# Expert blocks of 32 rows as four column groups in a one-core decoder trunk step

## The chip, the core and the metric

The kernel runs on one core of one Trainium2 chip. The time is the device time of that core in microseconds (us). Every product here is in f32; the trace shows each f32 product as two MATMUL records, so counts of records are twice the counts in the code.

## What is computed

One inference step of a decoder layer for 512 prompt tokens and 8 sample tokens (520 rows of 1024): a gated recurrent branch and a linear-attention branch, a merge, a layer norm, and then a mixture of experts. The change concerns the mixture alone:

```python
grp_logits = h @ w_grp + b_grp;  g_sel = argmax(grp_logits)          # 4 groups
sel_logits = (h @ w_exp + b_exp).reshape(N, 4, 8)[n, g_sel]          # 8 experts in the group
top_v, top_i = lax.top_k(sel_logits, 2)
e_id = g_sel * 8 + top_i;  e_w = softmax(top_v) * softmax(grp_logits)[g_sel]
y = sum over the 2 experts:  e_w * ((silu(h @ we_gate[e]) * (h @ we_up[e])) @ we_down[e])
```

There are 32 experts, with gate and up weights of 1024x512 and down weights of 512x1024, so 2 MB each and 6 MB an expert. 520 tokens make 1040 pairs of token and expert. With the reference's inputs its router gives the experts these counts, in order: 29, 84, 12, 7, 45, 22, 68, 117, 52, 33, 64, 10, 61, 60, 15, 19, 10, 7, 14, 8, 28, 15, 32, 24, 10, 29, 40, 10, 23, 44, 22, 26.

## The kernel before

The first part (projections, recurrences, merge, output projection, router) runs job by job, and the change leaves it alone up to the router's plan. VectorE then counts the pairs of each expert, cuts them into blocks of at most `CAP` rows, and gives each pair a block and a place in it. TensorE turns that into a table `idx` with one matmul per tile and choice (job `table`): for each block and place, which row of `hf_scratch` to gather and which row of `pair_scratch` to write. A second small job (`plan`) makes the table `plan` of register values: for each block the half of the weight ring that it uses and how many loads must have landed; for each load the expert and the block after which its slot is free.

The expert stage is a loop written for all engines, two blocks to an iteration (`two_blocks`), with `NBLK // 2` iterations; iterations past the last block fall through their `If`s. The count of blocks is in a register `n`. For a block b in slot j = b % 2 of all double buffers:

- GpSimd (`gather`) fetches the rows of block b + 2 by an indirect DMA into `xg[j]`, and (`scatter`) writes the result `yb[j]` of an earlier block to `pair_scratch`.
- TensorE, in this order: `gate_up(b)`, both products into one bank of PSUM; `transpose_rows` of block b + 1; `finish(b - 1)`, which calls `down`; the transposes of the product `act` of block b.
- ScalarE: silu of the gate, the copy of the transposed rows to `xT` for block b + 1, the copy of the transposed product to `acT`.
- VectorE: the product with the up half into `act`, and the copy of a result out of PSUM (`take_result`).
- The SP queue loads weights (`load_expert`) into a ring of two slots of three tiles. Expert e takes slot e % 2: gate and up wait until the last block of expert e - 2 is through `gate_up`, down until it is through `down`. SP works this list in order.

Before each `gate_up` and again before each `down` TensorE's own sequencer reads three values of `plan` for the block (`weights_of`), waits for the loads that they name, and takes one of two branches by the slot:

```python
lies, in0, in1 = weights_of(i * 2 + j)
for m in range(2):
    pe.wait_ge(we_in[m], in0 * 16)
    pe.wait_ge(we_in[3 + m], in1 * 16)
for slot in range(2):
    with pe.If(lies < 1 if slot == 0 else lies > 0):
        gate_up(j, slot)
```

In a block of 64 rows each of the two products of `gate_up` has 64 columns of the array to itself: gate goes to partitions 0 to 63 of the bank, up to 64 to 127, and `down` lays the two halves of its 1024 outputs in the same way. After the loop SP reads `pair_scratch` back, and the last layer norm follows.

## Time and profile before

| | us |
|---|---|
| median of 3 runs | 1518.23 (1515.2 to 1527.52) |
| span of the profiled execution, its own time in the trace | 1523.0 |
| first `gate_up` starts | 880.38 |
| last `down` ends | 1453.56 |

The trace has times from the start of the span. For the profiled execution there is no other time than its span; it lies between the highest run and the median. A row of TensorE in the timeline gives the start and the length of a run of instructions of one line, their count, and in square brackets how long the engine was idle before it and what ended that. Rows with PEldq are instructions of TensorE's sequencer (branches, register loads, waits), which are not counted as busy.

### The profile page before, as it was taken

To read this page: it belongs to the slowest core of one execution; us is meant where nothing else is said; L and a number is where in the kernel's file an instruction comes from. 1 tells how busy PE (TensorE), PEld (TensorE's weight loads), DVE (VectorE), ACT (ScalarE), POOL (GpSimd) and SP (SyncE) were. 2 spreads that over 40 slices of the span, in tenths; PEclk is the share of its full clock that TensorE was granted. 3 is DMA by queue.
4 is the path that set the end of the run, shared out by engine and by line. 5 is a ranking of instruction groups with operands and counts; after the bars stand their busy time and mean duration, and the time that the engine had idled before them with its cause. 6 is when DMAs were issued, how large, how long until landed. Compare 5 with 4: busy or idle time off the path is not lost.

```text
span 1523.0 us, 18481 instructions
## 1 busy us (share of the span) xinstructions
PE 1262.4 (83%) x6402; PEld 815.4 (54%) x6403; DVE 413.6 (27%) x704; ACT 307.3 (20%) x433; POOL 127.0 (8%) x203
## 2 busy tenths in 40 slices
PE   3899999999999999999987379798887977788710
PEld 3687878787878888888643223233332332233300
DVE  3326240423332260010386601111111111111156
ACT  3255550410000320000100012121211111111221
POOL 0100000000000000000000111111111111111134
PEclk9899999998878999999998579999998999889965
DMA  8744412124232213413003457996999999999631
GB/s 286 238 171 157 176 56 69 48 72 151 83 110 70 84 56 114 165 56 111 31 15 155 193 194 299 389 348 262 396 397 379 393 367 394 383 378 391 259 119 55
DMA packets 69930, 307.24 MB, mean 202 GB/s; under 512 B 10039, under 2 KB 18744, under 8 KB 56917
## 3 DMA queue, kind: packets, MB, share of 16 engines
q1 hardware_dynamic: 59786, 294.77, 50.5%
q0 software_dynamic: 6272, 10.14, 2.1%
q10 hardware_dynamic: 3820, 1.60, 0.4%
q8 instruction: 38, 0.62, 0.2%
q14 instruction: 14, 0.11, 0.0%
HBM read 298.35 MB, written 18.55 MB: 208 GB/s over the span
## 4 chain that ended last, share of the span: by engine, by line
PE 64%; DMA 18%; DVE 8%; issue 4%; ACT 3%; SPq 2%; ACTq 0%; POOL 0%; POOLq 0%; DVEq 0%; PEldq 0%
PE ps L1482 33%; DMA mem<-in_we_up 13%; PE ps L1750 12%; PE ps L1759 5%; PE ps L1709 3%; DMA mem<-in_w_mod 2%; PE ps L1639 2%; PE ps L1742 2%; PE ps L1636 1%; PE ps L1621 1%; DVE mem L1445 1%; PE ps L1647 1%; DMA mem<-in_we_gate 1%; DVE mem L1444 1%; PE ps L1515 1%
## 5 line engine op out<-in xcount | busy, mean ns | idle before, releaser
L1482 PE MATMUL ps<-mem 128*128 128x260 f32 (+1 forms) x2336 | 546.6, 396 | 10.3 <-ACT mem L813 3.9
L1482 PEld LDWEIGHTS ps<-mem 128*128 128x128 f32 (+1 forms) x2336 | 454.5, 196 | 95.3 <-issue 12.6
L1750 PE MATMUL ps<-mem 128*64 128x512 f32 x1120 | 286.7, 671 | 99.9 <-DMA mem<-in_we_up 78.4
L1750 PEld LDWEIGHTS ps<-mem 128*64 128x64 f32 x1120 | 89.7, 154 | 270.9 <-issue 270.9
L1424 DVE TENSOR_TENSOR mem<-mem,ps 64x512 f32<-64x512 f32 x35 | 24.1, 690 | 431.3 <-ACT mem L1002 431.3
L1759 PE MATMUL ps<-mem 128*64 128x512 f32 x560 | 129.2, 604 | 3.4 <-issue 3.4
L1002 ACT ACT_TABLE_LOAD x35 | 44.9, 1283 | 372.5 <-PE ps L1750 372.5
L1759 PEld LDWEIGHTS ps<-mem 128*64 128x64 f32 x560 | 37.5, 138 | 66.8 <-issue 64.5
L710 POOL DMA_INDIRECT pair_scratch<-mem x35 | 32.7, 934 | 458.2 <-DVE mem L1416 458.2
L1416 DVE COPY mem<-ps 64x512 f32<-64x512 f32 x70 | 48.1, 688 | 78.1 <-PE ps L1759 77.0
L1709 PE MATMUL ps<-mem 128*128 128x512 f32 x128 | 59.8, 628 | 0.0
L1742 PEld LDWEIGHTS ps<-mem 64*128 64x128 f32 x288 | 34.4, 200 | 32.6 <-issue 32.6
L931 ACT ACTIVATE mem<-ps,mem 128x520 f32<-128x520 f32 x16 | 11.1, 694 | 169.9 <-PE ps L1482 169.8
L1742 PE MATMUL ps<-mem 64*128 64x64 f32 x288 | 39.4, 278 | 4.0 <-DMA mem<-hf_scratch,mem 4.0
L651 POOL IOTA mem<- 128x4 int32 x1 | 0.1, 137 | 510.0 <-DVEq L1218 510.0
L1709 PEld LDWEIGHTS ps<-mem 128*128 128x128 f32 x128 | 25.4, 201 | 31.7 <-issue 31.6
L688 POOL DMA_INDIRECT mem<-hf_scratch,mem x37 | 35.9, 970 | 31.5 <-POOL mem L719 29.7
L1814 PEld LDWEIGHTS ps<-mem 64*128 64x128 f32 x140 | 19.4, 210 | 29.5 <-issue 29.5
L1238 DVE TENSOR_TENSOR mem<-mem,ps 128x520 f32<-128x520 f32 x8 | 5.6, 696 | 102.9 <-PE ps L1482 102.9
L906 ACT ACTIVATE mem<-ps,mem 128x520 f32<-128x520 f32 x8 | 5.6, 694 | 133.8 <-PE ps L1482 133.8
L1009 ACT ACTIVATE mem<-ps 128x256 f32<-128x256 f32 x35 | 13.5, 384 | 94.0 <-PE ps L1814 94.0
L1515 PE MATMUL ps<-mem 128*9 128x128 f32 x768 | 25.9, 292 | 5.2 <-DMA mem<-in_w_mod 5.2
(284 smaller groups left out, 988.7 us busy)
## 6 DMA issues: line engine op xcount, KB each, us to landing
mem<-in_we_gate SPq DMA_DIRECT2D x32, 2048.0 KB, 12.0
mem<-in_we_up SPq DMA_DIRECT2D x32, 2048.0 KB, 16.5
mem<-in_we_down SPq DMA_DIRECT2D x32, 2048.0 KB, 8.9
mem<-in_w_in SPq DMA_DIRECT2D x14, 2048.0 KB, 8.5
mem<-in_w_mod SPq DMA_DIRECT2D x12, 2048.0 KB, 12.0
out<-mem SPq DMA_DIRECT2D x13, 512.0 KB, 5.3
mem<-in_state_gla SPq DMA_DIRECT2D x8, 512.0 KB, 3.9
mem<-v_scratch SPq DMA_DIRECT2D x8, 512.0 KB, 4.3
```

The source lines that it names most:

```text
L688: pool.indirect_dma_start(xg[j][0:CAP, :], None, hf_dram, bass.IndirectOffsetOnAxis(ap=gidx[j][0:CAP, 0:1], axis=0), bounds_check=NT - 1, ...
L710: pool.indirect_dma_start(pair_dram, bass.IndirectOffsetOnAxis(ap=sidx[j][0:CAP, 0:1], axis=0), yb[j][0:CAP, :], None, bounds_check=PAIRS ...
L1002: sc.activation(sg[j][CAP:2 * CAP, :], ps[0:CAP, 2 + j, :], ACT.Silu).then_inc(sg_ready[j], 1)
L1416: v.tensor_copy(yb[j][0:CAP, q * 512:(q + 1) * 512], ps[CAP * q:CAP * q + CAP, 4 + j, :])\
L1424: v.tensor_tensor(act[j][0:CAP, :], sg[j][CAP:2 * CAP, :], ps[CAP:2 * CAP, 2 + j, :], ALU.mult)\
L1482: ins = pe.matmul(out[0:m, h, 0:HALF], w[:, k, col:col + m], src[:, k, h * HALF:(h + 1) * HALF], start=(k == 0), stop=(k == KD - 1))
L1515: pe.matmul(o, cs[:, k, :], w[:, k, g * P:(g + 1) * P], start=(k == 0), stop=False)
L1639: ins = pe.matmul(o, S[n % 2][:, h, d * P:(d + 1) * P], Q[:, h, cols], start=False, stop=True)
L1709: ins = pe.matmul(out[0:r, h, :], Z[:, k, i * P:i * P + r], wo[h][:, k, :], start=(k == 0), stop=(k == KD - 1))
L1742: ins = pe.transpose(ps[:, j, k * CAP:(k + 1) * CAP], xg[j][0:CAP, :].rearrange("s (p k) -> s k p", k=KD)[:, k, :], ident[0:CAP, 0:CAP])
L1750: ins = pe.matmul(ps[CAP * q:CAP * q + CAP, 2 + j, :], xT[j][:, k, :], ring[3 * slot + q][:, k, :], start=(k == 0), stop=(k == KD - 1))
L1759: ins = pe.matmul(ps[CAP * q:CAP * q + CAP, 4 + j, :], acT[j][:, k, :], wd[:, k, q * 512:(q + 1) * 512], start=(k == 0), stop=(k == 3))
```

## The change

A block has 32 rows instead of 64, the program is built for up to 64 blocks instead of 48, and SPLITS, the number of thresholds of the block count, goes from 9 to 17. In `gate_up` four column groups of 32 take a half of gate or up each (256 outputs), in `down` a quarter of the 1024 outputs each. Gathered rows lie as quarters: partition 32q + s holds quarter q (256 values) of row s, so `xg` and `yb` fill 128 partitions with 1 KB each, and the table repeats the indices for the four quarters (`piece` adds q). Two full transposes replace eight smaller ones, and two replace four for the product. The order of the rows of the weight tiles follows from that: a partition holds, of gate and up, four pieces of 4 KB that lie 512 KB apart in memory, and of down two pieces of 8 KB that lie 1 MB apart; before it held 16 KB in one piece.

```diff
-CAP = 64
+CAP = 32
+Q4 = 4
+DQ = D // Q4
+HE = DE // 2
-NBLK = 48
+NBLK = 64
-SPLITS = 9
+SPLITS = 17
...
-                to = ring[3 * slot + m]
-                if m < 2:
-                    sp.dma_start(to, w.rearrange("o (p k) n -> p (o k) n", p=P)).then_inc(we_in[3 * slot + m], 16)
-                else:
-                    sp.dma_start(to.rearrange("p k n -> p (k n)"), w.rearrange("o (p k) n -> p (o k n)", p=P))\
-                      .then_inc(we_in[3 * slot + m], 16)
+                to = ring[3 * slot + m].rearrange("p k n -> p (k n)")
+                q = Q4 if m < 2 else 2
+                sp.dma_start(to.rearrange("p (q w) -> p q w", q=q),
+                             w.rearrange("o (q p h) n -> p (o q) (h n)", q=q, p=P)).then_inc(we_in[3 * slot + m], 16)
...
-                pool.indirect_dma_start(xg[j][0:CAP, :], None, hf_dram,
-                                        bass.IndirectOffsetOnAxis(ap=gidx[j][0:CAP, 0:1], axis=0),
-                                        bounds_check=NT - 1, oob_is_err=False).then_inc(xg_in[j], 16)
+                pool.indirect_dma_start(xg[j][:], None, hf_dram.rearrange("t (q e) -> (t q) e", q=Q4),
+                                        bass.IndirectOffsetOnAxis(ap=gidx[j][:, 0:1], axis=0),
+                                        bounds_check=Q4 * NT - 1, oob_is_err=False).then_inc(xg_in[j], 16)
...
-                        sc.activation(sg[j][CAP:2 * CAP, :], ps[0:CAP, 2 + j, :], ACT.Silu).then_inc(sg_ready[j], 1)
+                        sc.activation(sg[j][2 * CAP:P, :], ps[0:2 * CAP, 2 + j, 0:HE], ACT.Silu).then_inc(sg_ready[j], 1)
...
-                for q in range(2):
-                    v.tensor_copy(yb[j][0:CAP, q * 512:(q + 1) * 512], ps[CAP * q:CAP * q + CAP, 4 + j, :])\
-                     .then_inc(y_ready[j], 1)
+                v.tensor_copy(yb[j][:], ps[:, 4 + j, 0:DQ]).then_inc(y_ready[j], 1)
...
-                ins = pe.matmul(out[0:CAP, 0, 0:2 * NBLK], place_oh[0:r, n, :], named[0:r, n].rearrange("p b c -> p (b c)"),
-                                start=(n == 0), stop=(n == 2 * TILES - 1))
+                for q in range(Q4):
+                    ins = pe.matmul(out[CAP * q:CAP * q + CAP, 0, 0:2 * NBLK], place_oh[0:r, n, :],
+                                    named[0:r, n].rearrange("p b c -> p (b c)"), start=(n == 0), stop=(n == 2 * TILES - 1))
...
-                for k in range(KD):
-                    for q in range(2):
-                        ins = pe.matmul(ps[CAP * q:CAP * q + CAP, 2 + j, :], xT[j][:, k, :], ring[3 * slot + q][:, k, :],
+                for h in range(2):
+                    ins = pe.transpose(ps[:, j, h * P:(h + 1) * P], xg[j].rearrange("s (p h) -> s h p", h=2)[:, h, :], ident[:])
+                ins.then_inc(xt_done[j], 1)
+
+            def gate_up(j, slot):
+
+                for k in range(KD):
+                    for q in range(Q4):
+                        ins = pe.matmul(ps[CAP * q:CAP * q + CAP, 2 + j, 0:HE], xT[j][:, k % 2, CAP * (k // 2):CAP * (k // 2) + CAP],
+                                        ring[3 * slot + q // 2][:, k, (q % 2) * HE:(q % 2 + 1) * HE],
                                         start=(k == 0), stop=(k == KD - 1))
...
                 for k in range(4):
-                    for q in range(2):
-                        ins = pe.matmul(ps[CAP * q:CAP * q + CAP, 4 + j, :], acT[j][:, k, :],
-                                        wd[:, k, q * 512:(q + 1) * 512], start=(k == 0), stop=(k == 3))
+                    for q in range(Q4):
+                        ins = pe.matmul(ps[CAP * q:CAP * q + CAP, 4 + j, 0:DQ], acT[j][:, k % 2, CAP * (k // 2):CAP * (k // 2) + CAP],
+                                        wd[:, k, q * DQ:(q + 1) * DQ], start=(k == 0), stop=(k == 3))
```

Three places show how the order on an engine changes. Lines of the changed kernel are a few higher than those of the kernel before. The first is TensorE in the loop, from the branch into `gate_up` of a block to the branch into `finish`. Before:

```order
L1796 COMPARE_AND_BRANCH
L1750 MATMUL ps<-mem 64x512 x16
L1796 UNCONDITIONAL_BRANCH
L1799 ISA
L1742 MATMUL ps<-mem 128x64 x8
L1788 UNCONDITIONAL_BRANCH
L1804 COMPARE_AND_BRANCH
```

The same place in the changed kernel:

```order
L1800 COMPARE_AND_BRANCH
L1753 MATMUL ps<-mem 32x256 x32
L1800 UNCONDITIONAL_BRANCH
L1803 ISA
L1746 MATMUL ps<-mem 128x128 x2
L1792 UNCONDITIONAL_BRANCH
L1808 COMPARE_AND_BRANCH
```

Sixteen matmuls of 64 columns become 32 of 32 columns and half the length, eight transposes become two, and the sequencer's own instructions stay. The second place is TensorE from the branch into `down` to the transposes of the product. Before:

```order
L1783 COMPARE_AND_BRANCH
L1759 MATMUL ps<-mem 64x512 x8
L1783 UNCONDITIONAL_BRANCH
L1809 COMPARE_AND_BRANCH
L1810 REGISTER_ALU
L1811 REGISTER_ALU
L1814 MATMUL ps<-mem 128x64 x4
```

In the changed kernel:

```order
L1787 COMPARE_AND_BRANCH
L1763 MATMUL ps<-mem 32x256 x16
L1787 UNCONDITIONAL_BRANCH
L1813 COMPARE_AND_BRANCH
L1814 REGISTER_ALU
L1815 REGISTER_ALU
L1818 MATMUL ps<-mem 128x64 x2
```

The matmuls of `down` double in number at half the length, the transposes halve in number. The third place is the SP queue, one expert's loads in the loop. Before:

```order
L587 ISA
L550 ISA
L550 DMA mem<-in_we_gate 128x4096
L550 DMA mem<-in_we_up 128x4096
L552 DMA mem<-in_we_down 128x4096
```

In the changed kernel:

```order
L589 ISA
L554 ISA
L554 DMA mem<-in_we_gate 128x4x1024
L554 DMA mem<-in_we_up 128x4x1024
L554 DMA mem<-in_we_down 128x2x2048
```

The loads stand in the same order with the same bytes, each partition's part now in four pieces or two.

## Rows read from the trace of the kernel before

**Rows 1.** Windows of the expert stage: us, busy us (instructions), granted clock, DMA share, GB/s.

```profile
880.38:1144.99 264.61, 222.26 (x1005) 85.64 (x1005) 33.73 (x49) 48.52 (x68) 37.65 (x66) 0.93 0.85 332
1144.99:1346.17 201.18, 163.13 (x720) 62.00 (x721) 24.79 (x36) 34.25 (x48) 25.70 (x46) 0.90 0.94 380
1346.17:1453.56 107.39, 85.79 (x376) 32.35 (x376) 12.39 (x18) 18.41 (x25) 14.91 (x26) 0.90 0.80 322
```

**Rows 2.** Timeline of TensorE, one block and the start of the next.

```profile
1016.40 7.09 PE L1750 MATMUL ps<-mem 128*64 128x512 f32 x32 [1.44 <-issue]
1023.42 1.09 PE L1742 MATMUL ps<-mem 64*128 64x64 f32 x8
1024.44 3.65 PE L1759 MATMUL ps<-mem 128*64 128x512 f32 x16
1028.03 0.69 PE L1814 MATMUL ps<-mem 64*128 64x64 f32 x4
1030.54 8.78 PE L1750 MATMUL ps<-mem 128*64 128x512 f32 x32 [1.82 <-issue]
```

**Rows 3.** Sequencer of TensorE by line: ns, first and last start, same block.

```profile
L1799 PEldq FUSED_REGOPS  x1: 42/42/42, 1019.0 to 1019.0; - x1
...
L1804 PEldq COMPARE_BRANCH  x1: 71/71/71, 1020.8 to 1020.8; - x1
...
L1783 PEldq COMPARE_BRANCH  x2: 78/148/218, 1023.6 to 1024.5; - x2
...
L1811 PEldq ALU_OP  x2: 32/32/32, 1012.5 to 1026.2; - x2
```

**Rows 4.** ScalarE and VectorE in the same block, timeline.

```profile
1023.59 1.28 ACT L1002 ACT_TABLE_LOAD   x1 [8.13 <-PE ps L1750]
...
1025.51 0.69 DVE L1424 TENSOR_TENSOR mem<-mem,ps 64x512 f32<-64x512 f32 x1 [9.62 <-ACT mem L1002]
```

**Rows 5.** Sequencer of TensorE around one `down` of the other slot.

```profile
L1783 PEldq COMPARE_BRANCH  x2: 68/148/228, 1251.5 to 1251.8; - x2
...
L1809 PEldq COMPARE_BRANCH  x1: 71/71/71, 1252.4 to 1252.4; - x1
```

**Rows 6.** TensorE by line and form: the earlier matmul in four column groups.

```profile
L1704 PE MATMUL ps<-mem 128*8 128x256 f32 x64 | 3.6, 379 | 0.0
```

**Rows 7.** Timeline of TensorE, `gate_up` of six blocks.

```profile
880.38 9.22 PE L1750 MATMUL ps<-mem 128*64 128x512 f32 x32 [3.14 <-issue]
...
1144.99 10.03 PE L1750 MATMUL ps<-mem 128*64 128x512 f32 x32 [4.52 <-DMA mem<-in_we_up]
...
1161.91 7.09 PE L1750 MATMUL ps<-mem 128*64 128x512 f32 x32 [1.66 <-issue]
...
1194.33 8.78 PE L1750 MATMUL ps<-mem 128*64 128x512 f32 x32 [1.91 <-DMA mem<-in_we_up]
...
1346.17 7.09 PE L1750 MATMUL ps<-mem 128*64 128x512 f32 x32 [1.06 <-issue]
...
1431.37 8.50 PE L1750 MATMUL ps<-mem 128*64 128x512 f32 x32 [5.01 <-DMA mem<-in_we_up]
```

**Rows 8.** Before the stage: the table's matmuls, and one VectorE instruction of the plan.

```profile
864.33 0.83 DVE L1363 TENSOR_TENSOR mem<-mem 128x640 f32<-128x640 f32 x1
...
867.35 3.65 PE L1727 MATMUL ps<-mem 128*64 128x96 f32 x20 [9.52 <-DVEq L1369]
```

**Rows 9.** DMA in 830 to 845 (16 KB pieces), and in 575 to 580 (2 KB pieces of `p_a`).

```profile
DMA packets 475, 6.44 MB, mean 430 GB/s; under 512 B 48, under 2 KB 48, under 8 KB 93
...
DMA packets 952, 1.96 MB, mean 392 GB/s; under 512 B 1, under 2 KB 1, under 8 KB 951
```

**Rows 10.** The end of the stage: the last `down`, and VectorE's branches after its last block.

```profile
1448.55 5.01 PE L1759 MATMUL ps<-mem 128*64 128x512 f32 x16 [3.44 <-issue]
...
L1421 DVEq COMPARE_BRANCH  x12: 56/56/63, 1454.1 to 1460.9; - x12
```

**Rows 11.** DMA issues: the gathers, median us to landing.

```profile
mem<-hf_scratch,mem POOLq DMA_INDIRECT x37, 9.3
```

More of the change, by code:

```diff
@@ L215, in build @@
         hfT = [area(B + WT + 1024 * j, KD, P) for j in range(2)]
-        xT = [area(Z0 + 512 * j, KD, CAP) for j in range(2)]
-        sg = [area(Z0 + 1024 + 512 * j, DE) for j in range(2)]
-        act = [area(Z0 + 2048 + 512 * j, DE) for j in range(2)]
-        acT = [area(Z0 + 3072 + 256 * j, 4, CAP) for j in range(2)]
-        xg = [area(A0 + 4160 + 1024 * j, D) for j in range(2)]
-        yb = [area(A0 + 4160 + 2048 + 1024 * j, D) for j in range(2)]
+        xT = [area(Z0 + 256 * j, 2, P) for j in range(2)]
+        sg = [area(Z0 + 512 + 256 * j, HE) for j in range(2)]
+        act = [area(A0 + 4160 + 1024 + 256 * j, HE) for j in range(2)]
+        acT = [area(A0 + 4160 + 1536 + 128 * j, 2, 2 * CAP) for j in range(2)]
+        xg = [area(A0 + 4160 + DQ * j, DQ) for j in range(2)]
+        yb = [area(A0 + 4160 + 512 + DQ * j, DQ) for j in range(2)]
         ln2 = area(A0, 2, D)
@@ L261, in build @@
         fmv = keep(TILES, 4)
+        piece = keep(1)
         wa2 = area(2 * WT + 2048, 512)
@@ L316, in build @@
         place_oh = area(Z0 + 1024, 2 * TILES, CAP)
-        block_oh = area(Z0 + 1024 + 640, 2 * TILES, NBLK)
-        named = area(Z0 + 1024 + 1120, 2 * TILES, NBLK, 2)
-        idx = area(Z0 + 3584, TW, 2).bitcast(I32)
+        block_oh = area(Z0 + 1024 + 320, 2 * TILES, NBLK)
+        named = area(Z0 + 1024 + 960, 2 * TILES, NBLK, 2)
+        idx = area(Z0 + 3500, TW, 2).bitcast(I32)
         gidx = [area(Z0 + 3700 + j, 1).bitcast(I32) for j in range(2)]
@@ L679, in _ @@
             for j in range(2):
-                link(pool.memset(xg[j][0:CAP, :], 0.0))
+                link(pool.memset(xg[j][:], 0.0))
             pool.wait_ge(idx_ready, 1)
@@ L1392, in _ @@
             await_job(v, ("table", 0))
-            link(v.tensor_scalar_add(idx[0:CAP, 0:NBLK, :],
-                                     slot_banks(("table", 0))[0:CAP, 0, 0:2 * NBLK].rearrange("p (b c) -> p b c", c=2), float(OOB)))
-            link(v.tensor_scalar(idx[0:CAP, NBLK:TW, :], blk_f[0:CAP, 0:2 * (TW - NBLK)].rearrange("p (b c) -> p b c", c=2),
+            link(v.tensor_scalar(idx[:, 0:NBLK, :], slot_banks(("table", 0))[:, 0, 0:2 * NBLK].rearrange("p (b c) -> p b c", c=2),
+                                 piece[:, 0:1], 0.0, ALU.add, ALU.add))
+            link(v.tensor_scalar(idx[:, NBLK:TW, :], blk_f[:, 0:2 * (TW - NBLK)].rearrange("p (b c) -> p b c", c=2),
                                  0.0, float(OOB), ALU.mult, ALU.add))
@@ L1757, in down @@
                 for k in range(4):
-                    for q in range(2):
-                        ins = pe.matmul(ps[CAP * q:CAP * q + CAP, 4 + j, :], acT[j][:, k, :],
-                                        wd[:, k, q * 512:(q + 1) * 512], start=(k == 0), stop=(k == 3))
+                    for q in range(Q4):
+                        ins = pe.matmul(ps[CAP * q:CAP * q + CAP, 4 + j, 0:DQ], acT[j][:, k % 2, CAP * (k // 2):CAP * (k // 2) + CAP],
+                                        wd[:, k, q * DQ:(q + 1) * DQ], start=(k == 0), stop=(k == 3))
                 ins.then_inc(dn_done, 1)
@@ L1812, in two_blocks @@
                         pe.sem_inc(pe_turns, 1)
-                        for k in range(4):
-                            ins = pe.transpose(ps[:, 6 + j, k * CAP:(k + 1) * CAP],
-                                               act[j][0:CAP, :].rearrange("s (p k) -> s k p", k=4)[:, k, :],
-                                               ident[0:CAP, 0:CAP])
+                        for h in range(2):
+                            ins = pe.transpose(ps[:, 6 + j, 2 * CAP * h:2 * CAP * (h + 1)],
+                                               act[j][0:2 * CAP, :].rearrange("s (p h) -> s h p", h=2)[:, h, :],
+                                               ident[0:2 * CAP, 0:2 * CAP])
                         ins.then_inc(tr_done[j], 1)
```

32 lines of the change are left out of this document (16 added, 16 removed).

## The prediction

> **What bounds the kernel now.** The change sits in the expert stage, from 880.38 to 1453.56, so I read that stage first by windows, then the timeline of TensorE, then its sequencer. The windows [rows 1] show two regimes. In the middle one, 201.18 us for twelve experts of one block each, the DMA engines are 0.94 busy at 380 GB/s: 16.8 us an expert, and TensorE waits for weights. In the first window, 264.61 us for experts 0 to 13 in 17 blocks, DMA is only 0.85 busy, since three experts have two blocks and hold their slot longer.
>
> How long a block takes when its weights are there is seen in [rows 2]: `gate_up` starts at 1016.40 and the next at 1030.54, so 14.1 us, of which the array works 12.3 and then sits idle 1.82, with no engine named as the cause. The sequencer's rows [rows 3] show the cause. It passes L1811 at 1026.2, and the next `gate_up` starts 4.3 us later; on the iteration before, 1012.5 to 1016.40, it is 3.9. In that time it ends the `If`, loops, reads three registers and takes the branch. What it waits for at L1811 is ScalarE and VectorE: `gate_up` ends at 1023.5, the table load runs from 1023.59 for 1.28, VectorE ends at 1026.20 [rows 4]. So a block is `gate_up` 7.1, plus 2.7 for silu and product, plus 4.1 of sequencer: 13.9. The array's work on `down` and the transposes (1.09, 3.65 and 0.69 [rows 2]) lies beside that and sets nothing. The same register work stands ahead of `down`: from L1804 at 1020.8 to L1783 at 1023.6, 2.8 us [rows 3], today hidden because `gate_up` is long and the sequencer runs ahead of the array.
>
> **How many blocks.** From the router's counts, 64 rows make 35 blocks and 32 rows make 47. Experts 0 to 13 go from 17 to 27, experts 14 to 25 stay at 12, experts 26 to 31 go from 6 to 8. The bytes of weights stay.
>
> **The new block, step by step.** (1) `gate_up`. The nearest row is the earlier matmul in four groups with the same length: 64 records in 3.6 us [rows 6], so the groups do run side by side, 0.053 us a record, and 64 records here take about 3.65. Its groups have 8 columns, here 32; from the loads of 64 columns, which stay hidden today, I take no extra.
>
> (2) The clock. A `gate_up` after 1.66 us of idle ran at full clock in 7.09, after 1.91 in 8.78, after 1.82 also in 8.78 [rows 2, 7]. The extra is 1.7 there and 2.9 in the row of 10.03. If the new block idles longer than that before each `gate_up` (step 5 says 3 us), each one pays about 1.7: 5.35. Bounds: 3.65 with no drop, 7.0 if the clock never rises.
>
> (3) How far ahead the sequencer gets. At L1799, 2.6 us into `gate_up`, all 32 records are issued, and the array has 4.5 of 7.1 us left, which is 21 records of 0.22 us. So about 21 records is the lead. In the new block 21 records are 1.1 us: the sequencer leaves `gate_up` 4.1 us after its start, needs about 0.4 for two transposes, and is at the branch of `finish` at 4.5.
>
> (4) The 2.8 us of register work now start there and end at 7.3, when the array has been done for 1.5 us. Then 32 records of `down` are issued. In [rows 5] 16 records are issued between 1251.8 and 1252.4, at most 0.03 us each, so 1.0 here, and with the branch L1811 comes at 8.85. Silu and product are ready by then (5.35 + 2.35 = 7.7; the two instructions are half as long).
>
> (5) Then the 4.1 us as today: 12.95 us a block. The array ends `down` near 9.4 and the transposes near 9.9 and idles 3 us. With the clock up throughout the same steps give 11.25, with the clock always low 13.65. A block of 32 rows then costs nearly what one of 64 costs, because what is halved is the array's part, and the sequencer's part is the same for each.
>
> **The sum, against the span of 1523.0.**
>
> - Before the stage: the table gets 80 records for 20, in four groups; 20 records took 3.65 [rows 8]. Side by side that is about +0.8, and the longer plan instructions on VectorE about +0.9, from 0.83 for 640 elements [rows 8]; the first transposes and copy give back 0.8. Together +0.9 (0 to +4).
> - Experts 0 to 13: 27 x 12.95 = 350, plus one wait for weights early on of some 3, is 353 against 264.6: +88. DMA alone would need 12 x 16.5 = 198, so TensorE sets the pace and both slots are full ahead of it.
> - Experts 14 to 25: the first two find weights in the ring (13 and 15.6 us), then DMA binds again at about 16.6: 195 against 201.2, so -6. The 16.6 is today's 16.8 with two opposite terms. The hand-over is faster, which closes part of the 6% in which DMA idles. Against it stand smaller pieces: 16 KB pieces moved at 430 GB/s, 2 KB pieces at 392 [rows 9], so 4 and 8 KB pieces cost between 0 and 1.4 us an expert; I take 0.5. Bounds of this term: -16 to +8.
> - From the first block of expert 26 to the last `gate_up`, today 1346.17 to 1431.37: 7 x 12.95 plus one wait of 3.4, 94 against 85.2: +9.
> - The tail from the last `gate_up` to the last `down`: 22.2 today, of which 5.0 for `down` at low clock [rows 7, 10]. The shorter `gate_up` and `down` give about -3.6.
> - The loop's end: 8 empty iterations instead of 6 on VectorE. Six take 1454.1 to 1460.9, so 1.25 each [rows 10]; of 2.5 more some hides behind the last scatter, and one copy replaces two: +0.7 (0 to +2.5).
>
> Gathers and scatters move the same bytes in four times as many pieces. I cost them at nothing: a gather lands in 9.3 us [rows 11] and is issued about two blocks ahead, 26 us; if it took twice that, it would still be in time. GpSimd's order stays, and the vector copies are shorter.
>
> Sum: 0.9 + 88 - 6 + 9 - 3.6 + 0.7 = +89 on 1523.0, so 1612. The median stands 4.8 below that span, so I carry the difference over: 1518 + 89 = 1607, I say 1606.
>
> **The rivals.** *The sequencer hides* (8 in 100). If the register work still lay behind the array, a block would take the array's time with today's pause before `gate_up`: 3.65 + 0.5 + 1.85 + 0.5 + 1.7 = 8.2. Experts 0 to 13 would take about 250 (221 plus waits for weights at experts 4, 6 and 12 and their slow restarts), -14; experts 14 to 25 about -3; the rest about -9 with a shorter tail: 1492, faster. It decides below some 9.5 us a block. For it speaks that the pairing of groups works [rows 6]; against it the 2.8 and 4.1 us that have no wait in them [rows 3]. The Trainium skill, "TensorEngine Tiling (Array Packing)", in its section on theoretical speedup, puts the gain for a stationary side of at most 32 columns at up to four times, against two at 64. By that rule the array's part halves, which is this rival; the rows with the sequencer's part speak against taking it for the block.
>
> *The clock stays up* (19 in 100): 11.25 a block gives 27 x 1.7 = 46 less for the first stretch and 8 less at the end, 1552. Against it: 3 us of idle before each `gate_up`, where 1.9 was enough [rows 7]. *The clock never rises* (14 in 100): 0.7 more on 34 blocks, 1630. *The transfers slow down* (5 in 100): pieces that lie far apart cost more than small ones, 1 us an expert and more on the twelve that DMA sets and the waits near them, 1620 to 1630. The Trainium skill, "DMA: Bandwidth & Descriptors", under its latency and other measured facts, reports that rows at pitches of large powers of two read slower, somewhat at 512 KiB and more at 2 MiB and above. Here the pieces of a partition lie 512 KB apart; the pieces of `p_a` lie just so and moved at 392 GB/s [rows 9], so the trace speaks against it. *The groups don't run side by side* (2 in 100): `gate_up` of 32 columns would take 13.7 us, and the time would pass 1750.
>
> **How the numbers follow.** The forecast, 1585 to 1620 around 1606, has the other 52 in 100. A change of under 1% (15 us) can hardly be told from none with runs that spread by 12 us. Faster by over 1%, under 1503: 5 in 100, most of the first rival. Within 1%: 5, its upper part. Slower: 90. The range reaches from 1545, just below the case of the high clock, to 1632, the case of the low clock: outside lie the first rival, the last, and parts of two others.
>
> **What would show it.** In the changed kernel: 47 table loads for silu; `gate_up` near 5.3 us; between the xT transposes and `down` an idle stretch of 1.5 us or more, and some 3 us before the next `gate_up` where no weights are awaited; blocks 12 to 14 us apart in experts 6 to 13; DMA clearly less busy than 0.85 there and above 0.94 in experts 16 to 25. The prediction is wrong if blocks follow each other within 10 us, or if the idle stretches end with a gather or a weight load.

## The result, and the profile after

The changed kernel takes 1533.4 us (median of 6 runs, 1526.8 to 1536.7) against 1519.7 for the kernel before in the same job: a ratio of 1.0083, interval 1.0051 to 1.0114 (1.0090 by the two medians). Run again in a later job, it stood at 1533.9 against 1517.3, 1.013 (1.0102 to 1.0158). So it is slower, as forecast, but by 14 to 17 us where 88 were forecast.

The profiled executions alone would mislead. That of the changed kernel was the fastest of its six (span 1525.1), that of before lay above its median (span 1523.0), so the spans differ by only 2.1. The terms below come from these two; the profile of the second job is set beside them.

The stage by windows, as in [rows 1] (us, busy us of PE, PEld, DVE, ACT and POOL, granted clock, DMA share, GB/s): experts 0 to 13, 14 to 25, then the last ones up to the end of the last `down`, and ten of the one-block experts alone:

```profile
877.01:1169.24 292.23, 183.38 (x2668) 105.88 (x2669) 22.45 (x53) 62.67 (x108) 63.97 (x104) 0.95 0.79 310
1169.24:1354.43 185.19, 100.28 (x1201) 51.72 (x1201) 10.17 (x24) 27.85 (x48) 31.76 (x52) 0.79 1.01 404
1354.43:1452.93 98.50, 58.79 (x832) 32.71 (x832) 6.79 (x16) 19.07 (x33) 18.59 (x30) 0.92 0.87 340
...
1196.06:1354.43 158.37, 85.78 (x1001) 43.52 (x1001) 8.47 (x20) 23.21 (x40) 24.81 (x40) 0.78 1.02 411
```

The first window went from 264.6 to 292.2 us although TensorE works less in it (183 against 222). The second went from 201.2 to 185.2, at 404 GB/s against 380. One block, on TensorE's timeline (the answer to [rows 2]):

```profile
1084.19 3.66 PE L1753 MATMUL ps<-mem 128*32 128x256 f32 x64 [2.32 <-issue]
1087.79 0.50 PE L1746 MATMUL ps<-mem 128*128 128x128 f32 x2
1089.84 1.94 PE L1763 MATMUL ps<-mem 128*32 128x256 f32 x32 [1.55 <-DMA mem<-in_we_down]
1091.70 0.45 PE L1818 MATMUL ps<-mem 64*128 64x64 f32 x2
1094.30 3.66 PE L1753 MATMUL ps<-mem 128*32 128x256 f32 x64 [2.15 <-issue]
```

The array works 6.5 us of 10.1 and pauses twice: 1.55 before `down` and 2.15 before the next `gate_up`. The first pause is put down to a weight load, but the sequencer's rows of the same block (the answer to [rows 3]; in order of time: end of `gate_up`'s branch, branch of `finish`, branch ahead of `down`, wait for the product, branch ahead of the next `gate_up`) say what it is:

```profile
L1803 PEldq FUSED_REGOPS  x1: 42/42/42, 1086.4 to 1086.4; - x1
...
L1808 PEldq COMPARE_BRANCH  x1: 71/71/71, 1086.6 to 1086.6; - x1
...
L1787 PEldq COMPARE_BRANCH  x2: 68/142/217, 1089.4 to 1089.7; - x2
...
L1815 PEldq ALU_OP  x1: 32/32/32, 1090.5 to 1090.5; - x1
...
L1800 PEldq COMPARE_BRANCH  x1: 71/71/71, 1094.2 to 1094.2; - x1
```

The sequencer never rests: 2.2 us to issue `gate_up`, 0.2, 2.8 of register work, 1.1 with the issue of `down`, 3.8 to the next `gate_up`. VectorE ends the product at 1090.1, 0.4 us before L1815 asks for it:

```profile
1089.68 0.42 DVE L1427 TENSOR_TENSOR mem<-mem,ps 64x256 f32<-64x256 f32 x1 [7.61 <-ACT mem L1007]
```

So a block is as long as its instruction stream, 10.1 us. The product of [rows 4] was what the sequencer waited for before; it no longer is.

The clock is the surprise. `gate_up` of three blocks, with the idle time before each:

```profile
1012.15 3.66 PE L1753 MATMUL ps<-mem 128*32 128x256 f32 x64 [2.69 <-issue]
...
1115.25 5.35 PE L1753 MATMUL ps<-mem 128*32 128x256 f32 x64 [2.73 <-issue]
...
1196.06 6.45 PE L1753 MATMUL ps<-mem 128*32 128x256 f32 x64 [7.46 <-DMA mem<-in_we_up]
```

After 2.69 us of idle time the first ran at a granted clock of 1.00; the second, after nearly the same 2.73, at 0.68. In the kernel before, 1.82 us had been enough to slow a block [rows 2]. But its trace also has a block that stayed at full clock after 1.87:

```profile
940.16 7.09 PE L1750 MATMUL ps<-mem 128*64 128x512 f32 x32 [1.87 <-issue]
```

So even there the length of the pause did not put slow and fast blocks in order. Of the 27 blocks of experts 0 to 13 of the changed kernel only 5 are slow. In the profile of the second job 9 are, and that window takes 297.8 us: the same blocks, the same pauses, another draw of the clock.

The forecast's terms against these two traces (us):

| term | forecast | measured |
|---|---|---|
| planning, from the first rank matmuls to the first `gate_up` | +0.9 | +0.3 (25.2 to 25.5) |
| experts 0 to 13 | +88 | +27.6 (second profile +33.2) |
| experts 14 to 25 | -6 | -16.0 (second -15.5) |
| expert 26 to the last `gate_up` | +9 | -0.8 (84.4 against 85.2) |
| last `gate_up` to the end of the last `down` | -3.6 | -8.1 (14.1 against 22.2) |
| from there to the end | +0.7 | +2.7 (72.2 against 69.4) |

They sum to +5.7; what lies ahead of the stage, which nothing changed, ran 3.7 us shorter in this execution, and that leaves the 2.1 of the spans. With the second profile the stage and all after it are 12.2 us longer than before, which is near the medians' 13.7 and 16.5.

### The profile page after: what moved, and what is told of

Read it like the earlier page. It is cut to its first block, busy times and chain, and to the rows that moved or that the text cites. A ratio compares the mean times of both kernels' runs of the same rounds, so it can differ in the third digit from the quotient of the medians.

```text
span 1525.1 us, 24902 instructions
## 1 busy us (share of the span) xinstructions
PE 1130.2 (74%) x9056; PEld 822.8 (54%) x9057; DVE 382.6 (25%) x693; ACT 316.3 (21%) x481; POOL 162.3 (11%) x255
## 4 chain that ended last, share of the span: by engine, by line
PE 59%; DMA 18%; issue 9%; DVE 8%; ACT 3%; SPq 1%; ACTq 0%; DVEq 0%; POOL 0%; POOLq 0%; PEldq 0%
PE ps L1485 32%; DMA mem<-in_we_up 9%; PE ps L1753 8%; PE ps L1763 5%; DMA mem<-in_we_down 5%; PE ps L1712 3%; PE ps L1642 2%; PE ps L1639 2%; DMA mem<-in_w_mod 2%; DMA mem<-in_we_gate 1%; PE ps L1624 1%; PE ps L1518 1%; DVE mem L1448 1%; PE ps L1650 1%; PE ps L1746 1%
## 5 line engine op out<-in xcount | busy, mean ns | idle before, releaser
L1753 PE MATMUL ps<-mem 128*32 128x256 f32 x3008 | 208.8, 439 | 160.8 <-DMA mem<-in_we_up 95.1
L1753 PEld LDWEIGHTS ps<-mem 128*32 128x32 f32 x3008 | 110.4, 126 | 243.3 <-issue 204.9
L1763 PE MATMUL ps<-mem 128*32 128x256 f32 x1504 | 95.4, 390 | 73.7 <-issue 55.9
L1427 DVE TENSOR_TENSOR mem<-mem,ps 64x256 f32<-64x256 f32 x47 | 19.9, 423 | 450.9 <-ACT mem L1007 450.9
L1763 PEld LDWEIGHTS ps<-mem 128*32 128x32 f32 x1504 | 50.5, 111 | 104.0 <-issue 83.5
L714 POOL DMA_INDIRECT pair_scratch<-mem x47 | 48.1, 1024 | 417.8 <-DVE mem L1420 417.8
L692 POOL DMA_INDIRECT mem<-hf_scratch,mem x49 | 51.7, 1055 | 41.8 <-POOL mem L724 40.0
L1420 DVE COPY mem<-ps 128x256 f32<-128x256 f32 x47 | 20.0, 425 | 92.2 <-PE ps L1763 92.2
L1014 ACT ACTIVATE mem<-ps 128x128 f32<-128x128 f32 x47 | 13.0, 278 | 104.8 <-PE ps L1818 104.8
L1518 PE MATMUL ps<-mem 128*9 128x128 f32 x768 | 27.6, 305 | 4.4 <-DMA mem<-in_w_mod 4.4
L1639 PE MATMUL ps<-mem 64*128 64x64 f32 x128 | 29.9, 328 | 0.0
L1642 PE MATMUL ps<-mem 128*128 128x64 f32 x112 | 28.9, 347 | 0.0
## 6 DMA issues: line engine op xcount, KB each, us to landing
mem<-in_we_gate SPq DMA_DIRECT2D x32, 2048.0 KB, 10.7
```

The source lines that it names most:

```text
L692: pool.indirect_dma_start(xg[j][:], None, hf_dram.rearrange("t (q e) -> (t q) e", q=Q4), bass.IndirectOffsetOnAxis(ap=gidx[j][:, 0:1], axi ...
L714: pool.indirect_dma_start(pair_dram.rearrange("r (q e) -> (r q) e", q=Q4), bass.IndirectOffsetOnAxis(ap=sidx[j][:, 0:1], axis=0), yb[j][:] ...
L1420: v.tensor_copy(yb[j][:], ps[:, 4 + j, 0:DQ]).then_inc(y_ready[j], 1)
L1427: v.tensor_tensor(act[j][0:2 * CAP, :], sg[j][2 * CAP:P, :], ps[2 * CAP:P, 2 + j, 0:HE], ALU.mult)\
L1518: pe.matmul(o, cs[:, k, :], w[:, k, g * P:(g + 1) * P], start=(k == 0), stop=False)
L1639: ins = pe.matmul(o, v_tok[q:q + 64, tile, hd * P:(hd + 1) * P], attm[n % 2][q:q + 64, h, :], start=True, stop=(n == 0))
```

## The experiments

All times are medians, each ratio against the kernel before in the same job. Slow blocks are counted among the 27 of experts 0 to 13 (`gate_up` over 3.8 us).

**The changed kernel again.** No edit.

> The changed kernel once more, unedited, as the control for the other runs of this job. Its first profiled execution was the fastest of six and showed a span only 2 us above that of before, while the medians lie 13.7 apart. If that difference is TensorE's clock, which varies from one execution to the next, a second profile with a longer span has the same blocks, 10.1 to 10.7 us apart where weights are there, and more gate_up that take 5.35 instead of 3.66 us, 1.7 each: some 6 more for 10 us. If the stage itself is longer in the typical execution (transfers, waits for weights), the gate_up starts are further apart with gate_up at 3.66. Ratio to before 1.005 to 1.012 either way.

1533.9, 1.013 (1.0102 to 1.0158), span 1531.2. The first case held: blocks 9.9 to 10.9 us apart where the clock was up, and 9 slow `gate_up` instead of 5. Two neighbours there:

```profile
1024.50 3.66 PE L1753 MATMUL ps<-mem 128*32 128x256 f32 x64 [2.37 <-issue]
1034.94 5.35 PE L1753 MATMUL ps<-mem 128*32 128x256 f32 x64 [2.46 <-issue]
```

**Eight register loads a block.**

```diff
+                        pe.value_load(plan[0:1, bass.ds(b + BLK_IN0, 1)], min_val=1, max_val=NE),
...
-                lies, in0, in1 = weights_of(i * 2 + j)
+                lies, in0, in1, again = weights_of(i * 2 + j)
+                pe.wait_ge(we_in[2], again * 16)
...
+                        pe.wait_ge(we_in[0], again * 16)
```

> One register load more before gate_up and one more before down, each with a wait that is already met: 8 loads a block instead of 6. Sequencer theory (TensorE's instruction stream sets the pace of a block, and the array waits for it): each load costs some 0.74 us of the block, so blocks go from 10.2 to 11.7 us; 25 of the 27 blocks of experts 0 to 13 and 5 at the end are so paced, 30 x 1.5 = 44 us more, a ratio of 1.035 to 1.04 to before; nothing in the stretch where DMA binds. ScalarE theory (table load, silu, product and copies set the pace) and transfer theory (weights set it): the loads lie beside that, within 5 us of the changed kernel, 1.01. Clock theory, as the prediction had it (more idle time before gate_up lowers the clock): gate_up falls to 5.35 in most blocks on top of the loads, since the idle time before it grows from 2.2 to 2.9 us, and the ratio passes 1.06.

1613.7, 1.0663 (1.0627 to 1.0699): 80 us above the changed kernel, so ScalarE and transfers do not set the pace; and more than loads alone explain. One block:

```profile
1143.98 5.35 PE L1753 MATMUL ps<-mem 128*32 128x256 f32 x64 [2.88 <-DMA mem<-in_we_gate]
1149.26 0.50 PE L1746 MATMUL ps<-mem 128*128 128x128 f32 x2
1152.48 1.94 PE L1763 MATMUL ps<-mem 128*32 128x256 f32 x32 [2.72 <-issue]
1154.35 0.45 PE L1821 MATMUL ps<-mem 64*128 64x64 f32 x2
1157.33 5.35 PE L1753 MATMUL ps<-mem 128*32 128x256 f32 x64 [2.53 <-issue]
```

Blocks are 13.35 us apart here: 10.1, twice 0.75 for the loads, and 1.7 for the clock. 23 of 27 are slow. Sequencer and clock both count, and this block is nearly the one that was forecast for the changed kernel.

**Two loads a block**, kept in registers until `down`.

```diff
...
-                        lies, in0, in1 = weights_of(i * 2 + j)
-                        for m in range(2):
-                            pe.wait_ge(we_in[m], in0 * 16)
-                            pe.wait_ge(we_in[3 + m], in1 * 16)
+                        lies = weights_of(i * 2 + j, j)
                         for slot in range(2):
                             with pe.If(lies < 1 if slot == 0 else lies > 0):
+                                have = loaded(i * 2 + j, j, slot)
+                                for m in range(2):
+                                    pe.wait_ge(we_in[3 * slot + m], have * 16)
                                 gate_up(j, slot)
```

> The changed kernel with two register loads a block instead of six: the slot, and inside the branch the count of that slot alone; both are kept in registers until the block's down. Sequencer theory: a block falls by 4 x 0.74 less some 0.2 for moves, from 10.2 to about 7.4 us, which is under the 15.9 us an expert that the transfers need; then DMA binds from the first expert to the last, experts 0 to 13 take some 222 us instead of 292, and the whole goes to 1455 to 1475, a ratio of 0.96 to 0.97. ScalarE theory: no change, 1.01. Transfer theory (blocks of the first stretch wait for weights): no change either. Clock theory: the array idles less, so the clock has no more reason to fall.

1522.6, 1.0041 (1.0023 to 1.006): 11 us gained instead of 60 to 80. The loads are gone, and the clock took their place: all 27 `gate_up` are slow.

```profile
1024.20 5.35 PE L1753 MATMUL ps<-mem 128*32 128x256 f32 x64 [2.30 <-issue]
1029.48 0.51 PE L1746 MATMUL ps<-mem 128*128 128x128 f32 x2
1029.91 1.93 PE L1763 MATMUL ps<-mem 128*32 128x256 f32 x32
1032.03 0.42 PE L1828 MATMUL ps<-mem 64*128 64x64 f32 x2 [0.18 <-DVE mem L1427]
1035.13 5.35 PE L1753 MATMUL ps<-mem 128*32 128x256 f32 x64 [2.68 <-issue]
```

The pause before `down` has gone; the transposes of act now wait for VectorE; the pause before `gate_up` is 2.0 to 2.8 us, much as in the changed kernel (1.6 to 2.7 in most blocks), where the clock stayed up. So the length of that pause does not decide. Nor does the idle time of a whole block: here it is 2.9 us of 10.9 (0.18 and 2.68), in the block of the changed kernel shown above 3.7 of 10.1, and that one kept its clock. The theory of the sequencer alone fell with this run: the block is `gate_up`, silu and product, and then the sequencer's way from the wait to the next `gate_up`, with `gate_up` at one of two prices.

**The kernel before with the same two loads.** The same edit.

> The kernel before with the same two loads a block. Sequencer theory: of its block of 13.9 us, gate_up 7.1, silu and product 2.7 and the stretch up to the next gate_up 4.1, only the last gets shorter, by one load less a move, 0.65 us; the three loads before down lie behind gate_up. 17 blocks of experts 0 to 13 and some of the last: 10 to 14 us less, a ratio of 0.991 to 0.993. So blocks of 32 rows would beat blocks of 64 by 40 us once the loads are few, where they lose by 13 with six. If register loads are not the reason, both kernels gain the same or nothing.

1498.7, 0.9888 (0.985 to 0.9926), 18.6 us less, more than the 10 to 14 expected. Experts 0 to 13 gave 7.8; the stretch bound by DMA, for which nothing had been expected, gave 6.0 (195.2 against 201.2): its ten one-block experts ran at 16.3 us each.

**Two loads, fetched early.**

```diff
...
+            def fetch(b, j):
+                pe.reg_mov(regs[j][0], pe.value_load(plan[0:1, bass.ds(b + BLK_SLOT, 1)], min_val=0, max_val=3 * WT))
+                pe.reg_mov(regs[j][1], pe.value_load(plan[0:1, bass.ds(b + BLK_IN0, 1)], min_val=1, max_val=NE))
...
+                        fetch(i * 2 + (j + 1), 1 - j)
                         pe.wait_ge(act_ready[j], i + 2)
...
```

> The changed kernel with two register loads a block, and these moved: TensorE's sequencer reads the next block's slot and count between down and the transposes of act, where it otherwise waits for VectorE's product (1.3 us in the run with two loads a block). Before gate_up only the loop, the waits and the branch are left, 1.6 us instead of 3.2. Theory now: a block takes gate_up, then 2.3 us to the product, then the sequencer's way to the next gate_up; and gate_up costs 3.66 or some 5.2 us as the clock falls or not before it. With the clock up a block takes 3.7 + 2.3 + 1.6 = 7.6 us, DMA binds all along, and the time is 1455 to 1475, a ratio of 0.96 to 0.97. With the clock down 9.1 to 9.4 us: 27 blocks take some 255 instead of 292, and the time is 1490 to 1500. Rival, the pace is set by transfers or gathers alone: no change from 1523, the time of two loads a block.

1482.6, 0.9759 (0.9717 to 0.9801): the fastest of all, between the two cases. Two blocks where weights were there, and ten one-block experts as a window:

```profile
1020.74 3.66 PE L1753 MATMUL ps<-mem 128*32 128x256 f32 x64 [0.79 <-issue]
1024.33 0.50 PE L1746 MATMUL ps<-mem 128*128 128x128 f32 x2
1024.77 1.93 PE L1763 MATMUL ps<-mem 128*32 128x256 f32 x32
1027.26 0.42 PE L1825 MATMUL ps<-mem 64*128 64x64 f32 x2 [0.56 <-DVE mem L1427]
1028.56 3.66 PE L1753 MATMUL ps<-mem 128*32 128x256 f32 x64 [0.88 <-issue]
```

```profile
1152.82:1311.18 158.36, 83.83 (x1000) 45.08 (x1001) 8.48 (x20) 23.21 (x40) 24.82 (x40) 0.72 1.02 411
```

A block takes 7.8 us, and now even experts 0 to 13 (245.8 us) wait for weights at four places, 2.8 us or more each. That is the block of the rival in which the sequencer hides (8.2 us, 1492): it takes the register work out of the way to get there.

**The kernel before with early loads.** The same edit.

> The kernel before with the same two early loads. By the same theory its block is 7.1 + 2.7 + 1.7 = 11.5 us instead of 13.9, 17 x 11.5 = 196 us in experts 0 to 13, below what the transfers need at 16.4 to 16.8 us an expert, so DMA binds there too, some 235 us instead of 265: 1485 to 1492, a ratio near 0.98. If the changed kernel with early loads stands below that by 15 us or more, halving the blocks is worth something once the sequencer is out of the way; if not, transfers alone decide both.

1488.9, 0.9798 (0.9758 to 0.9839), as expected. Where weights are there its array works without a pause:

```profile
1002.70 7.09 PE L1750 MATMUL ps<-mem 128*64 128x512 f32 x32
1009.72 1.09 PE L1742 MATMUL ps<-mem 64*128 64x64 f32 x8
1010.74 3.65 PE L1759 MATMUL ps<-mem 128*64 128x512 f32 x16
1014.32 0.69 PE L1821 MATMUL ps<-mem 64*128 64x64 f32 x4
```

12.2 us for 64 rows against 7.8 for 32, yet the two kernels are only 6 us apart, under the 15 set as the mark. With the sequencer out of the way transfers set most of what is left in both: in experts 14 to 25 the DMA engines are 0.98 (kernel before) and 1.02 busy; in experts 0 to 13, where the block still counts, 0.88 and 0.90.

**Four loads a block**, two before `gate_up` and two before `down`: the loads of the counts moved into the branch, as in the run with two, without keeping them.

> The changed kernel with four register loads a block: two before gate_up and two before down (the slot, and in the branch its own count). It tells whether the clock or the loads decided the run with two loads, whose gate_up took 5.0 to 5.4 us nearly everywhere with the same 2.0 to 2.7 us of idle time before it as in the changed kernel, whose gate_up took 3.66. Here the idle time before gate_up would be some 1.4 us and that before down 0.8. If idle time before gate_up decides, the clock stays up, a block takes 8.7 to 9.0 us and the time is 1485 to 1495. If the clock is up only where the array also pauses before down, it falls here as well: 10.3 to 10.7 us a block and 1520 to 1530.

1505.2, 0.9901 (0.9869 to 0.9933): between the two cases. 11 of 27 are slow, blocks 8.5 to 9.1 us apart where the clock was up and some 10.5 after a slow one. Neither pure rule holds.

**Small pieces alone, in the kernel before.** The order of the activations is left as it was, so the experts' results are not those of the layer; the time is what counts here.

```diff
-                to = ring[3 * slot + m]
-                if m < 2:
-                    sp.dma_start(to, w.rearrange("o (p k) n -> p (o k) n", p=P)).then_inc(we_in[3 * slot + m], 16)
...
+                to = ring[3 * slot + m].rearrange("p k n -> p (k n)")
+                q = 4 if m < 2 else 2
+                sp.dma_start(to.rearrange("p (q w) -> p q w", q=q),
+                             w.rearrange("o (q p h) n -> p (o q) (h n)", q=q, p=P)).then_inc(we_in[3 * slot + m], 16)
```

> The kernel before with only the new layout of the expert weights: pieces of 4 KB for gate and up and 8 KB for down, in place of 16 KB. The rows of the weights come in another order than the activations, so the expert outputs are not the reference's. The prediction's term: small pieces cost 0 to 1.4 us an expert, 0.5 taken, so 0 to 17 us more on the twelve experts that DMA sets, 1519 to 1536. Rival: the pieces move faster and are the reason why an expert takes 15.9 us in the changed kernel against 16.8: 10 to 15 us less, 1503 to 1508. If the faster hand-over of the changed blocks is the reason, this run stays within 5 us of before, and its rate in that stretch stays near 380 GB/s.

1522.1, 1.0007 (0.9984 to 1.003; one of ten runs took 4297 us and is not in the ratio). Ten one-block experts as a window, first in the kernel before, then in this run:

```profile
1178.59:1346.17 167.58, 135.55 (x600) 51.59 (x601) 20.66 (x30) 28.54 (x40) 21.26 (x38) 0.90 0.95 382
...
1172.06:1340.58 168.52, 137.38 (x600) 52.16 (x601) 20.66 (x30) 28.55 (x40) 22.70 (x40) 0.90 0.98 382
```

16.85 us an expert against 16.76, both at 382 GB/s: the layout by itself hardly moves the time, though the DMA engines are 0.98 busy for it instead of 0.95. So the changed kernel's 15.8 at 411 must come from its blocks. That these free the slot sooner was not measured by itself, but it fits the kernel before with fewer loads, whose blocks got shorter and which reached half of it (16.3).

**Eight loads, with the pauses filled** by matmuls of no use.

```diff
+            def fill(j, count):
+                for _ in range(count):
+                    pe.matmul(ps[:, 2 + j, 256:384], ident[:], ident[:], start=True, stop=True)
...
                         transpose_rows(1 - j)
+                        fill(1 - j, 6)
...
                         ins.then_inc(tr_done[j], 1)
+                        fill(j, 10)
```

> The changed kernel with the two extra loads a block, as in the run of eight loads, and matmuls of no use in the array's idle time: 6 of 128x128 after the xT transposes and 10 after the transposes of act, into columns of a bank that nobody reads, some 1.5 and 2.5 us at full clock. In the run of eight loads gate_up took 5.35 us in most blocks and blocks came 13.3 us apart. If those 1.7 us are the clock's answer to the idle array, gate_up goes back to 3.66, blocks to 11.6 and the time from 1614 to 1560 to 1570, although the array has more to do. If the clock has nothing to do with it, or the filler only adds to the array's work, the time is 1614 or more.

1627.4, 1.0732 (1.0704 to 1.0761). The clock did as expected, 4 of 27 slow instead of 23. The time did not:

```profile
1143.49 3.66 PE L1757 MATMUL ps<-mem 128*32 128x256 f32 x64 [2.02 <-issue]
1147.08 0.50 PE L1750 MATMUL ps<-mem 128*128 128x128 f32 x2
1147.42 1.50 PE L1745 MATMUL ps<-mem 128*128 128x128 f32 x12
1150.25 1.93 PE L1767 MATMUL ps<-mem 128*32 128x256 f32 x32 [1.33 <-issue]
1152.12 0.45 PE L1826 MATMUL ps<-mem 64*128 64x64 f32 x2
1152.50 2.50 PE L1745 MATMUL ps<-mem 128*128 128x128 f32 x20
```

After the filler the array still pauses 1.33 and 2.14 us. The instruction stream has to pass the filler before it comes to the loads. From the semaphore increment ahead of the transposes of act to the loop's end the sequencer takes 1.7 us for transposes and filler, where the changed kernel took 0.2 for the transposes (1090.6 to 1090.8):

```profile
L1824 PEldq EVENT_SEMAPHORE  x1: 51/51/51, 1151.1 to 1151.1; - x1
...
L1833 PEldq ALU_OP  x1: 32/32/32, 1152.8 to 1152.8; - x1
```

So the filler pushed the pauses back instead of filling them: 13.65 us a block.

**Two loads, with the pause filled**: 8 of the same matmuls after the transposes of act.

> The changed kernel with two loads a block, 1523 us, with 8 such matmuls after the transposes of act, 2 us of the 2.0 to 2.7 us of idle time before gate_up. There gate_up took 5.0 to 5.4 us in nearly every block, so four loads less a block had brought only 11 us. If the clock is why, gate_up takes 3.66, a block 8.7 to 9.0 instead of 10.4 us, and the time falls to 1475 to 1490. If not, 1523 or more.

1498.1, 0.9876 (0.9853 to 0.9899). 4 of 27 slow instead of 27 (one of the four in two parts): 24 us gained by work of no use, though not the 33 to 48 expected. Blocks are 9.3 us apart instead of 10.6, which is 1.3 and not the 1.4 to 1.7 expected, since many of the slow `gate_up` had taken 5.0 us and not 5.35; experts 0 to 13 fell from 291.0 to 266.7 us, the whole of the gain. So the clock had eaten 24 us of what the run with two loads could have gained. The rest of its missing gain is the way through silu, product and the sequencer, of which the early loads take a part.

**Blocks of 32 rows alone, in the kernel before** (the tables' places in memory follow their size).

```diff
-NBLK = 48
+NBLK = 64
+ROWS32 = 32
...
-            link(pool.iota(ii[:, 0:SPLITS], pattern=[[CAP, SPLITS]], base=0, channel_multiplier=0))
+            link(pool.iota(ii[:, 0:SPLITS], pattern=[[ROWS32, SPLITS]], base=0, channel_multiplier=0))
...
-            link(v.scalar_tensor_tensor(place[:], q1[:], -float(CAP), r1[:], ALU.mult, ALU.add))
+            link(v.scalar_tensor_tensor(place[:], q1[:], -float(ROWS32), r1[:], ALU.mult, ALU.add))
```

> The kernel before with its blocks cut at 32 rows and nothing else: 47 blocks instead of 35, each on tiles of 64 columns half empty, two column groups, pieces of 16 KB. By the block of before, 13.9 us: experts 0 to 13 take 27 x 13.9 and a wait, some 380 instead of 265 us, the last experts 7 x 13.9 and a wait, some 105 instead of 85, planning and the loop's end 3 more: 1650 to 1660. Against that the changed kernel's 1533 shows what the four groups give: 120 us on 34 blocks, 3.5 each. If the weights set the pace of the first stretch, the extra blocks cost far less: under 1560.

1654.1, 1.0916 (1.088 to 1.0952). Experts 0 to 13 took 382.2 us, the last ones 102.8. So the change is the sum of two large parts: twelve more blocks cost 137 us, and the shorter block gives 121 back.

**No silu.** `ACT.Copy` in place of `ACT.Silu` in the changed kernel: the experts are computed without it.

> The changed kernel with ScalarE copying the gate instead of taking its silu, so the expert outputs lack the silu, and no table needs to be loaded in each block. Sequencer theory: in the changed kernel the product is ready 0.4 us before TensorE's sequencer asks for it, so nothing changes, 1528 to 1540. ScalarE theory (1.3 us of table load in each block set the pace): 34 blocks x 1.3 = 44 us less, 1490.

1528.8, 1.0084 (1.0061 to 1.0108); the table loads of the blocks are gone, experts 0 to 13 take 292.2 us, as in the changed kernel. ScalarE does not set the pace.

**Three semaphore increments more** before `gate_up`'s loads.

```diff
+                        for _ in range(3):
+                            pe.sem_inc(pe_turns, 1)
                         lies, in0, in1 = weights_of(i * 2 + j)
```

> The changed kernel with three semaphore increments, which nobody waits for, before the register loads ahead of gate_up: some 0.3 us more of sequencer in a block, so 2.3 to 3.0 us of idle time there instead of 2.0 to 2.7. If the clock answers to the length of that pause alone, it must stay up as far as some 2.7 us, since it did in the changed kernel; then a few more gate_up are slow and the time is 1533 + 30 x 0.3 = 1542, with the longest pauses slow 1545 to 1555. If the changed kernel's clock stayed up because its pauses happened to come in a favourable rhythm, this small shift is enough to make a third or more of the blocks slow: 1555 to 1580.

1570.6, 1.0373 (1.035 to 1.0395), 37 us more than the changed kernel for 0.3 us of sequencer a block. 20 of 27 slow:

```profile
1050.26 5.35 PE L1753 MATMUL ps<-mem 128*32 128x256 f32 x64 [2.89 <-issue]
...
1062.05 5.05 PE L1753 MATMUL ps<-mem 128*32 128x256 f32 x64 [2.40 <-issue]
```

Slow after 2.16 and 2.40 us, which the changed kernel bore at full clock. The changed kernel's high clock was a narrow place.

**One load more before `gate_up`, and one less.** The first adds `again` as in the run with eight loads, there alone; the second takes the branch's own count there, as in the run with four loads.

> The changed kernel with one register load more before gate_up and none more before down: seven a block, idle time before gate_up 2.8 to 3.5 us, before down 1.5 as in the changed kernel. By length of the pause: slow in nearly all blocks, 30 x (0.75 + 1.7) = 73 us more, about 1605. By rhythm: slow in some, fast in others, between 1555 (load alone) and 1605.

> The changed kernel with one register load less before gate_up and three before down as before: five a block, idle time before gate_up 1.3 to 2.0 us. By length of the pause: gate_up stays at 3.66, blocks fall from 10.3 to 9.6 us and the time from 1533 to 1510 to 1514. By rhythm: part of the blocks get slow though their pause is shorter than in the changed kernel, and the time lies between 1515 and 1560.

One more: 1579.2, 1.0418 (1.04 to 1.0437), 21 of 27 slow, with full clock in one block after 3.66 us and slow in another after 2.50. One less: 1514.4, 0.999 (0.9967 to 1.0013), 8 of 27 slow, some after 1.85 us (two of the eight, of 4.0 and 4.1 us, follow a slow `down` without a pause). The first lies where the theory of the rhythm put it, halfway; the second lies on the border between the two, and by the theory of the pause every `gate_up` would have stayed at 3.66. From five loads to six to seven the time goes 1514, 1534, 1579: a load costs some 20 us by itself, and over twice that where the clock goes with it.

## Why the prediction was wrong

**What bounds the kernel now** was right: the sequencer's part of a block is the same for 32 rows as for 64. The control by 47 old blocks, which took 382 us in experts 0 to 13, bears out the 13.9 us a block; the count of 27 blocks was right too.

**Step 1**, `gate_up` at 3.65, was right to 0.01.

**Step 2 failed, and it is the largest error.** It let each `gate_up` fall to 5.35 us because it would idle longer than 1.8 us, a limit read from blocks of 14 us [rows 2, 7]. The block at 940.16 of the same trace, at full clock after 1.87, already spoke against that limit. The pauses came, somewhat shorter than the 3 us of step 5 (1.6 to 2.7 in most blocks); the fall did not: 5 of 27 were slow, 9 in the second profile. 18 to 22 blocks at 1.7 are 31 to 37 of the 61 us by which experts 0 to 13 were overrated. The mechanism is real: it shows in the runs with eight loads, with two, and with 0.3 us more, and filling the pause undid it. What was wrong is the rule that the pause's length before `gate_up` decides. It orders neither the blocks within a run nor the runs, and the idle time of a whole block does no better. What does decide stays open; that the changed kernel hit upon a favourable pattern is what the run with three increments suggests, and no run shows the pattern's rule.

**Steps 3 to 5** were right in kind and 0.9 us too long together: with the clock up they gave 11.25, and 9.9 to 10.7 were measured, 10.3 on average between 960 and 1104. In the block shown above, 10.1 long: the sequencer came to `finish` 0.4 us sooner than said, the issue of 32 records of `down` took 0.45 less (the 16 records of [rows 5] gave no good price for these), the way back 3.8 for 4.1. The 2.8 us of register work stood there to the tenth. Over 25 blocks 0.9 us is 23 us, about the rest of the 61. The rival "the clock stays up", 19 in 100 and 1552, was the case that came; with 0.9 us less on its 34 blocks it would have said 1521. To that the 5 to 9 blocks that were slow after all add 9 to 15 us, and two waits for weights that were longer than reckoned (9.4 and 9.5 us of idle time before `gate_up` at 947.69 and 1405.74) some 8; the other terms of the table take 13 back. That gives 1525 to 1531, near the 1533 that came. (In its own sum the rival took 8 us off at the end, where 7 blocks at 1.7 are 12.)

**Experts 14 to 25** were mis-sized: -16 instead of -6. The term took 0.5 us an expert for small pieces, which the run with the pieces alone puts at 0.1, and too little for the hand-over: 15.8 us an expert were reached, in a range that allowed it (-16 to +8).

**The last experts and the tail** follow from the same two errors, +9 against -0.8 and -3.6 against -8.1; the last `down` took 2.85 us instead of 5.01. **Gathers at nothing** held: the gathers of the changed kernel land in 5.8 us against the 9.3 of [rows 11], by the page's line of it:

```profile
mem<-hf_scratch,mem POOLq DMA_INDIRECT x49, 5.8
```

**The signs for being wrong** were set too far off: the number missed, and yet most blocks came more than the stated 10 us apart (9.9 to 10.7). The sign that did fail is `gate_up` near 5.3. The direction was right for the reason given; the range began 12 us above the result because only one of its cases, at the bound, had the clock up, and none had the block shorter as well.

## What to carry to other kernels

When a change makes more and smaller pieces of work, price the instruction stream of a piece first (register loads, waits, branches), since it does not shrink with the piece; then take loads out of it or move them to where the stream waits anyway. Here that was worth 31 us in the kernel before and 51 in the changed one, while the change by itself cost 14. Give the clock two prices and both a fair chance when a loop pauses for 1.5 to 3 us in each round: in such a loop 0.3 us of code was worth 37 us, and two executions of one kernel differed by 6 us in one stretch.

## What the hardware showed that was not expected

- The clock's response to pauses is not in order of their length. In blocks of 10 to 13 us, `gate_up` ran at full clock after up to 2.73 us in the changed kernel and after 3.66 in one block of the run with seven loads. In the run with two loads all 27 were slow, with pauses from 2.01 us on. The Trainium skill, "TensorE: Matmul & The Clock Gate", in its part 1 on the warm-up, says that the same kernel shows differing numbers of slow matmuls from run to run. The two profiles of the changed kernel differ in this way, 5 and 9 slow `gate_up` of 27.
- Pieces of 4 KB that lie 512 KB apart and of 8 KB that lie 1 MB apart read at 411 GB/s with the DMA engines 1.02 busy; in the kernel before they kept the 382 GB/s of the 16 KB pieces, at 0.98 busy instead of 0.95. The Trainium skill, "DMA: Bandwidth & Descriptors", under latency and other measured facts, reports slower copies where the rows of the partitions lie large powers of two apart. No run here tests that: neighbouring partitions lie side by side here, and only the pieces of one partition are far apart.
- A register load costs the sequencer some 0.75 us, of which the load itself is 0.30: in the block of the changed kernel shown above the three ahead of `down` start at 1087.1, 1087.8 and 1088.6 and take 0.30 to 0.31 each. The address, the assertion and the gaps between them are the rest.
